# Attention outputs stored feature by feature, one pass that normalises them, and two modulation vectors of layer 0 formed on TensorE, in a two-layer hybrid encoder

## The chip, the cores and the metric

The kernel runs on one core of a Trainium2 chip. Its time is the device time of one execution in microseconds (us). The engines are TensorE (PE; its weight loads are PEld), VectorE (DVE), ScalarE (ACT), GpSimd (POOL) and SyncE (SP), which issues every DMA here.

## The reference, cut to what matters

Two sequences of 256 tokens with 1,024 features go through two layers. A layer modulates an RMS norm of x with vectors made from a conditioning vector c, projects it, and runs two groups of attention heads: group a has 8 query heads over 2 key and value heads of width 64, group b has 8 heads whose queries and keys are 96 wide, 64 without and 32 with a rotary position, the rotary key being shared by the heads. Each group's output (512 features) is RMS-normalised, and both go through one output projection. A channel mixer follows.

```
mod = silu(c) @ w_ada[l] + b_ada[l]                       # six vectors of 1024: shift, scale, gate, twice
h = rms_norm(x, g_attn) * (1.0 + scale_a) + shift_a
q_a, k_a, v_a, c_q, c_kv, k_r = split(h @ w_in)
o_a = softmax(q_a k_a^T * 64**-0.5) v_a                   # after head norm and rotation of q_a, k_a
q_b = rms_norm(c_q, g_cq) @ w_uq ; kv = rms_norm(c_kv, g_ckv) @ w_ukv
o_b = softmax([q_nope, rope(q_rope)] [k_nope, rope(k_r)]^T * 96**-0.5) v_b
x = x + gate_a * (concat(rms_norm(o_a, g_out_a), rms_norm(o_b, g_out_b)) @ w_o)
h = rms_norm(x, g_ffn) * (1.0 + scale_f) + shift_f
val, gate = split(conv3(h @ w_up)) ; x = x + gate_f * ((silu(gate) * val) @ w_down)
```

## The kernel before

**Numbers.** Each weight product is made of three one-pass matmuls (`product`, L614, L615, L620): a weight and an activation are each split into a rounded part, hi, and the remainder, lo, in the type fp32r. Attention itself runs on plain fp32 matmuls, which the trace shows as two matmuls and two weight loads each; a transpose is one.

**Weights.** SP loads 89 slots of 128 x 1,024 numbers a layer through a ring of four. ACT makes w_hi (L1117, `split_hi`), POOL makes w_lo in four quarters (L535), PE consumes. A slot of a ring is loaded again when POOL has read it and split again when PE has released it.

**Modulation vectors.** 11 vectors of 8 slots each are formed on DVE: a slot of `ada_raw` times silu(c), with a sum over its columns, for both sequences. A slot in full width takes two instructions (L1387), one in halves four (L1424). `ada_plan` says after which step of DVE's program how many slots are taken. Key ("unit", i) is unit i of the attention loop, ("wo", m) tile m of the output projection, ("up", g, i) and ("down", g, m) the tiles of the channel mixer, whose 22 tiles are in groups of 8, 8 and 6. SP loads slots of `ada_raw` through a ring of four of its own.

**Attention.** After the input projections, group b's queries are expanded token by token (L614 with ct_hi as the stationary operand, 384 columns), and their rotation is done by POOL (L579 to L588), which also copies the rotary key to all heads. Then 16 units follow, each of one pair of heads and one sequence: eight of group a, eight of group b. The loop keeps several units in flight. In a pass of it PE transposes the queries of the next unit (`fill`, L887 for a, L892 for b), multiplies them by the keys (`scores`, L917; for a the two heads use the upper and lower 64 rows of the array), transposes the probabilities of the unit before (`prob_transposes`, L931) and multiplies those of two units before by the values (`outputs`, L950). There the transposed probabilities are the stationary operand and the values move, 64 columns and one of ones, whose product is the sum of the exponentials. DVE takes the maxima (L1758) and divides the outputs by their sums (L1767, L1771). ACT copies the queries (L1278, L1280), takes the exponentials (L1307) and copies the transposed probabilities (L1296).

**End of attention.** `o_sb` is stored by token. ACT squares it by token (`stats`), DVE scales it, PE transposes it (L662), ACT and DVE split it into hi and lo (L1136, L1557), and `out_tile` multiplies it. Tiles 0 to 3 have 512 columns. Tiles 4 to 7 follow in halves by sequence (`norm_tail`), so that the sums of squares for the next norm hide behind them. DVE adds each tile to x (`update_x` L1593, `update_half` L1578) and sums the squares that ACT takes (`add_square`, L1570). A half needs a bank that an earlier update has freed.

**The order.** Each engine's program is written out by hand and the engines meet by semaphores; `plan_banks` deals the PSUM banks.

## Time and profile before

| | |
|---|---|
| median of 3 runs | 1193.37 us (1190.86 to 1193.6) |
| profiled execution | 1194.76 us, span 1193.0 us |
| mean granted TensorE clock | 0.986 of full speed |
| attention of layer 0, first query expansion to last 512-column output product | 91.6 to 223.5 us |
| the same of layer 1 | 670.5 to 792.1 us |
| DMA | 151.55 MB, mean 127 GB/s |

A busy share says how much of a stretch an engine had an instruction in flight. Matmuls overlap, so the spacing of their starts, and not their length, says what one costs. Where PE waited, its rows carry a bracket with the idle time and what ended it.

### The profile page before, as it was taken

To read this page: it belongs to the slowest core of one execution; us is meant where nothing else is said; L and a number is where in the kernel's file an instruction comes from. 1 tells how busy PE (TensorE), PEld (TensorE's weight loads), DVE (VectorE), ACT (ScalarE), POOL (GpSimd) and SP (SyncE) were. 2 spreads that over 40 slices of the span, in tenths; PEclk is the share of its full clock that TensorE was granted. 3 is DMA by queue.
4 is the path that set the end of the run, shared out by engine and by line. 5 is a ranking of instruction groups with operands and counts; after the bars stand their busy time and mean duration, and the time that the engine had idled before them with its cause. 6 is when DMAs were issued, how large, how long until landed. Compare 5 with 4: busy or idle time off the path is not lost.

```text
span 1193.0 us, 18770 instructions
## 1 busy us (share of the span) xinstructions
PE 1165.8 (98%) x6288; PEld 997.4 (84%) x6288; DVE 728.9 (61%) x1481; ACT 534.5 (45%) x866; POOL 568.4 (48%) x768
## 2 busy tenths in 40 slices
PE   9999999999999999999999999999999999999997
PEld 6897887998888888888789979889888888888886
DVE  5878986767766677757666438746775134412345
ACT  5347675254431344234354677635543234422432
POOL 2487500655655445644665540054555544454462
PEclk9999997999999999999999999999999999999998
DMA  9743333423445444544433202222343322332322
GB/s 350 307 168 116 92 103 107 141 72 132 174 139 207 133 166 176 194 141 176 141 110 119 75 1 89 89 89 71 124 141 106 106 86 90 106 106 74 102 89 71
DMA packets 43979, 151.55 MB, mean 127 GB/s; under 512 B 5122, under 2 KB 7810, under 8 KB 43908
## 3 DMA queue, kind: packets, MB, share of 16 engines
q1 hardware_dynamic: 43908, 150.64, 36.6%
q8 instruction: 40, 0.66, 0.2%
q14 instruction: 31, 0.25, 0.1%
HBM read 148.52 MB, written 2.10 MB: 126 GB/s over the span
## 4 chain that ended last, share of the span: by engine, by line
PE 46%; issue 24%; POOL 15%; POOLq 6%; DVE 6%; DVEq 2%; ACT 1%; ACTq 0%
POOL w_lo L535 14%; PE ps L614 14%; PE ps L620 14%; PE ps L615 14%; POOLq L536 5%; DVE ada_prod L1387 2%; DVEq L1389 1%; DVE nmx L1758 1%; PE ps L749 1%; PE ps L950 1%; PE ps L738 1%; PE ps L718 0%; DVE ada_prod L1608 0%; DVE o_sb L1771 0%; PE ps L726 0%
## 5 line engine op out<-in xcount | busy, mean ns | idle before, releaser
L535 POOL TENSOR_TENSOR w_lo<-w_raw,w_hi 128x256 fp32r<-128x256 f32 x712 | 532.1, 779 | 599.3 <-ACT w_hi L1117 575.7
L614 PE MATMUL ps<-h_hi,w_hi 128*128 128x512 f32 (+1 forms) x960 | 349.7, 364 | 4.2 <-DVEq L1561 2.2
L615 PE MATMUL ps<-h_lo,w_hi 128*128 128x512 f32 (+1 forms) x960 | 347.3, 362 | 0.0
L620 PE MATMUL ps<-h_hi,w_lo 128*128 128x512 f32 (+1 forms) x960 | 347.2, 362 | 0.0
L1117 ACT CAST w_hi<-w_raw 128x1024 fp32r<-128x1024 f32 x178 | 183.2, 1047 | 183.8 <-PE ps L614 183.6
L614 PEld LDWEIGHTS ps<-h_hi,w_hi 128*128 128x128 f32 x960 | 181.7, 189 | 36.8 <-DVEq L1561 3.8
L1809 DVE SCALAR_TENSOR_TENSOR u_sb<-ps,par,u_sb 128x510 f32<-128x510 f32 x176 | 131.7, 748 | 123.2 <-ACT u_sb L1345 110.2
L620 PEld LDWEIGHTS ps<-h_hi,w_lo 128*128 128x128 f32 x960 | 181.7, 189 | 27.5
L615 PEld LDWEIGHTS ps<-h_lo,w_hi 128*128 128x128 f32 x960 | 181.8, 189 | 27.2
L614 PE MATMUL ps<-a_hi,w_hi 128*128 128x512 f32 (+1 forms) x400 | 146.6, 366 | 3.3 <-DVEq L1595 2.4
L620 PE MATMUL ps<-a_hi,w_lo 128*128 128x512 f32 (+1 forms) x400 | 145.6, 364 | 0.0
L615 PE MATMUL ps<-a_lo,w_hi 128*128 128x512 f32 (+1 forms) x400 | 145.5, 364 | 0.0
L1424 DVE SCALAR_TENSOR_TENSOR ada_prod<-ada_raw,ps 128x512 f32<-128x512 f32 x192 | 124.2, 684 | 7.1 <-issue 0.9
L1345 ACT ACTIVATE u_sb<-ps,par 128x512 f32<-128x512 f32 x88 | 67.3, 773 | 109.0 <-PE ps L620 109.0
L1593 DVE SCALAR_TENSOR_TENSOR x<-ps,mod,x 128x256 f32<-128x256 f32 x96 | 42.1, 480 | 101.9 <-PE ps L620 100.8
L1387 DVE SCALAR_TENSOR_TENSOR ada_prod<-ada_raw,c_all 128x1024 f32<-128x1024 f32 x64 | 89.1, 1392 | 5.2 <-issue 1.2
L614 PEld LDWEIGHTS ps<-a_hi,w_hi 128*128 128x128 f32 x400 | 75.5, 189 | 17.9 <-issue 5.3
L620 PEld LDWEIGHTS ps<-a_hi,w_lo 128*128 128x128 f32 x400 | 75.5, 189 | 11.9
L615 PEld LDWEIGHTS ps<-a_lo,w_hi 128*128 128x128 f32 x400 | 75.5, 189 | 11.8
L1349 ACT ACTIVATE sil<-u_sb 128x512 f32<-128x512 f32 x44 | 27.8, 632 | 112.4 <-DVEq L1814 112.4
L614 PE MATMUL ps<-w_hi,h_hi 128*128 128x512 f32 (+2 forms) x192 | 67.2, 350 | 1.1 <-DVE h_lo L1651 0.9
L620 PE MATMUL ps<-w_hi,h_lo 128*128 128x512 f32 (+2 forms) x192 | 66.1, 344 | 0.0
(160 smaller groups left out, 1372.6 us busy)
## 6 DMA issues: line engine op xcount, KB each, us to landing
w_raw<-w_slots SPq DMA_DIRECT2D x178, 512.0 KB, 3.5
ada_raw<-ada_slots SPq DMA_DIRECT2D x88, 512.0 KB, 3.8
shift<-shift_slots SPq DMA_DIRECT2D x8, 512.0 KB, 13.2
x_tok<-x_rows SPq DMA_DIRECT2D x4, 512.0 KB, 9.6
x<-x_t SPq DMA_DIRECT2D x4, 512.0 KB, 13.7
y_t<-x SPq DMA_DIRECT2D x3, 512.0 KB, 2.9
y_t<-x SPq DMA_DIRECT2D x1, 256.0 KB, 3.0
y_t<-x SPq DMA_DIRECT2D x2, 128.0 KB, 2.7
```

The costliest lines, as they stand in the source:

```text
L535: nc.gpsimd.tensor_tensor(w_lo[:, j, c], w_raw[:, j, c], w_hi[:, j, c].bitcast(F32), ALU.subtract)
L536: nc.gpsimd.drain()
L614: hh = mm(out, stat[0], mov[0], start=first, stop=False)
L615: hl = mm(out, stat[0], mov[1], start=False, stop=False)
L620: return mm(out, stat[1], mov[0], start=False, stop=last)
L1117: nc.scalar.copy(w_hi[:, j, :], w_raw[:, j, :]).then_inc(hi_done, 1)
L1345: A(u_sb[:, e, half, :], ps[:, bank(key), :], ACT.Identity, bias=par[:, L, bass.ds(ft + PC_CB, 1)], scale=par[:, L, bass.ds(ft + (PC_CW + ...
L1349: A(sil[:, e, :], u_sb[:, e, 1, :], ACT.Silu).then_inc(sil_ready, 1)
L1387: V.scalar_tensor_tensor(out=ada_prod[:], in0=ada_raw[:, j % 4, :], scalar=1.0, in1=c_all[:, s, :], op0=ALU.mult, op1=ALU.mult, accum_out= ...
L1424: V.scalar_tensor_tensor(out=ada_prod[:, 512 * s:512 * s + 512], in0=ada_raw[:, q % 4, 512 * t:512 * t + 512], scalar=1.0, in1=ps[:, 6 + s ...
L1593: V.scalar_tensor_tensor(out=xs, in0=ps[:, bank(key), c], scalar=gate, in1=xs, op0=ALU.mult, op1=ALU.add)
L1809: V.scalar_tensor_tensor(out=u3[:, :, dst:dst + SEQ - 1], in0=p3[:, :, src:src + SEQ - 1], scalar=par[:, L, bass.ds(at + (PC_CW + tap * 2 ...
```

## The change

**Outputs by feature.** `outputs` swaps its operands: the values (64 columns) are stationary, the transposed probabilities move (256 columns), and the two heads of a pair use the left and right 64 columns of the array. The result has features in the partitions and is copied to `o_t` by DVE. The sums of the exponentials now come from ACT with each exponential (`accum_out`), and DVE divides the probabilities by them before they are transposed (`scale_rows`). A probability is transposed two passes after its scores, its output comes three passes after.

**One normalising pass.** POOL squares and adds `o_t` unit by unit; PE sums over partitions (`group_sums`), ACT takes roots, DVE inverts, PE spreads the result over all partitions (`group_spread`), DVE scales `o_t` once (`output_scaled`), ACT rounds, DVE subtracts. There is no transpose of outputs. Group a's part of output tiles 0 to 3 is multiplied ahead of group b's.

**Group b by feature.** Queries are expanded with the weights stationary (512 columns), with rotary columns and swapped ones beside each other; DVE multiplies these by a table. A score of group b is the sum of two matmuls of 64 rows each. The `fill` of group b and POOL's rotation are gone. The four rotary parts (kr_pad) are made by DVE.

**Modulation vectors.** The gate and shift of layer 0's attention and mixer (16 slots) are formed on PE in units 1 to 8 (`stream_products`: 32 stationary columns, four groups of columns; `stream_select`). The other slots move in the plan.

```diff
-ORDER = [(0, SCALE_A), (0, GATE_A), (0, SHIFT_F), (0, SCALE_F), (0, GATE_F),
+ORDER = [(0, SCALE_A), (0, SCALE_F), (0, GATE_A), (0, SHIFT_F), (0, GATE_F),
+READY = [(0, SCALE_A), (0, GATE_A), (0, SHIFT_F), (0, SCALE_F)] + ORDER[4:]
+STREAMED = (2, 3)
+N_PE = KD * len(STREAMED)
-HALVED = (4, 5, 6, 7, 8, 10)
+HALVED = (4, 5, 6, 7, 8, 9, 10)
...
-    plan = [(("in", 1), 6, 2), (("in", 2), S_UQ, 2)]
-    plan += [(("unit", i), S_WO - 1, 1) for i in range(NP + 1)]
-    plan += [(("wo", m), S_WO + m, 1) for m in range(1, TAIL)]
-    ups = [[1] * 8, [1, 2, 1, 2, 1, 2, 1, 1], [2, 2, 1, 1, 1, 0]]
+    plan = [(("in", 1), 6, 2), (("in", 2), S_UQ, 1), (("in", 3), S_UQ, 1)]
+    plan += [(("stream", i), S_WO - 1, 1) for i in range(N_PE)]
+    plan += [(("wo", m), S_WO + m, 1) for m in range(TAIL)]
+    ups = [[1, 2, 1, 2, 1, 2, 1, 2], [2, 2, 1, 2, 1, 2, 1, 2], [2, 2, 2, 2, 1, 0]]
...
-    plan += [((1, "unit", i), SLOTS + S_WO - 1, 1) for i in (7, 8, 9, 10, 11, 13, 14, 15)]
...
+                def add_squares(j):
+
+                    group, s, _ = PAIRS[j]
+                    k, c = pair_tile(j), slice(s * SEQ, (s + 1) * SEQ)
+                    total = (ssum if group == "a" else ssq_b)[:, c]
+                    pool.wait_ge(o_done, NP * L + j + 1)
+                    if k % 4 == 0:
+                        nc.gpsimd.tensor_tensor(total, o_t[:, k, c], o_t[:, k, c], ALU.mult)
+                    else:
+                        nc.gpsimd.tensor_tensor(o_sq[:, 0, :], o_t[:, k, c], o_t[:, k, c], ALU.mult)
+                        nc.gpsimd.drain()
+                        nc.gpsimd.tensor_tensor(total, total, o_sq[:, 0, :], ALU.add)
+                    nc.gpsimd.drain()
+                    pool.sem_inc(o_summed, 1)
...
+                for n in range(HEADS):
+                    j = slot(L, S_UQ + n // 4)
+                    key = ("uq", n)
+                    wait_free(pe, L, key)
+                    for k in range(2):
+                        at = (n % 4 * 2 + k) * P
+                        last = product(ps[:, bank(key), :], [r[:, j, at:at + P] for r in (w_hi, w_lo)],
+                                       [r[:, k, :] for r in (ct_hi, ct_lo)], k == 0, k == 1,
+                                       {0: 2, 4: 1}.get(n, 0) * int(k == 0))
+                    last.then_inc(full[bank(key)], 1)
...
+                        if group == "a":
+                            parts = [(q_t[:, j % 2, q * P:q * P + P], ka_t[:, c])]
+                        else:
+                            p, at = heads[0] // 2, s * SEQ + q * P
+                            parts = [(qn[:, p, at:at + P], kn[:, p, c]), (qr[:, p, at:at + P], kr_t[:, c])]
+                        for n, (st, mv) in enumerate(parts):
+                            for u in range(2):
                                 r = slice(64 * u, 64 * u + 64)
-                                st, mv = q_t[r, j % 2, 0, q * P:q * P + P], ka_t[r, s * SEQ:(s + 1) * SEQ]
-                            else:
-                                st = q_t[0:QK_B, j % 2, u, q * P:q * P + P]
-                                mv = kb_t[0:QK_B, heads[u], s * SEQ:(s + 1) * SEQ]
-                            last = mm(ps[:, S_BANK[j % 2] + u, q * SEQ:(q + 1) * SEQ], st, mv, start=True, stop=True)
+                                last = mm(ps[:, S_BANK[j % 2] + u, q * SEQ:(q + 1) * SEQ], st[r], mv[r], start=n == 0,
+                                          stop=n == len(parts) - 1)
...
+                    if L == 0 and j < 4 * len(STREAMED):
+                        stream_select(j)
                     pe.wait_ge(pt_ready, NP * L + j + 1)
-                    for u in range(2):
-                        for q in range(2):
-                            for k in range(2):
-                                v = va[:, 2 * s + k, u, :] if group == "a" else vb[:, 2 * s + k, heads[u], :]
-                                c = (2 * u + q) * VW
-                                last = mm(ps[:, O_BANK, c:c + VW], prob_t[:, j % 2, u, k, q * P:q * P + P], v,
-                                          start=(k == 0), stop=(k == 1))
+                    for k in range(2):
+                        for u in range(2):
+                            v = va[:, 2 * s + k, u, :] if group == "a" else vb[:, 2 * s + k, heads[u], :]
+                            last = mm(ps[64 * u:64 * u + 64, O_BANK, 0:SEQ], v, prob_t[:, j % 2, u, k, :],
+                                      start=(k == 0), stop=(k == 1))
                     last.then_inc(o_full, 1)
...
+                    pe.wait_ge(part_taken, h)
+                    for r in range(2):
+                        k = K_PE + 2 * h + r
+                        pe.wait_ge(ada_landed[k % 4], 16 * (k // 4 + 1))
+                        for g in range(4):
+                            last = mm(ps[32 * g:32 * g + 32, QT_BANK, 0:SEQ], c_pad[:, 4 * r + g, :],
+                                      ada_raw[:, k % 4, g * SEQ:(g + 1) * SEQ], start=r == 0, stop=r == 1)
+                        last.then_inc(ada_streamed, 1)
...
+                    pe.wait_ge(part_taken, h + 1)
+                    for f in range(2):
+                        at = h % 4 * 2 * NSEQ + f * NSEQ
+                        last = mm(stream_sums(h // 4)[:, at:at + NSEQ], part_sb(h)[:, f * P:f * P + P], sel, start=True,
+                                  stop=True)
+                    last.then_inc(stream_full, 1)
+
...
+                    if i == NP + 1:
+                        out_part(L, 0, (0, 1))
+                        group_sums(1)
                     if 0 <= i - 2 < NP:
-                        outputs(i - 2)
-                    if i >= NP:
-                        for k in range(2):
-                            output_transposes(L, 2 * (i - NP) + k)
-                for m in range(2):
-                    out_tile(L, m, range(KD // 2), int(m == 0))
-                for k in range(KD // 2, KD):
-                    output_transposes(L, k)
-                for m in range(2):
-                    out_tile(L, m, range(KD // 2, KD), int(m == 1))
-                for m in range(2, TAIL):
-                    out_tile(L, m, range(KD), 1)
+                        prob_transposes(i - 2)
+                    if L == 0 and 0 <= i - 1 < 4 * len(STREAMED):
+                        stream_products(i - 1)
+                out_part(L, 0, (2, 3))
+                group_spread(1)
+                outputs(NP - 1)
+                out_part(L, 1, range(KD // 2))
+                group_sums(2)
+                out_part(L, 2, range(KD // 2))
+                group_spread(2)
+                out_part(L, 3, range(KD // 2))
+                for m in range(TAIL):
+                    out_part(L, m, range(KD // 2, KD), int(m > 0))
                 norm_tail(2 * L + 1, lambda m, s, release: half_out(L, m, s, release))
...
-                split_hi(L, S_WO + 3)
+                              ACT.Exp, bias=nmx[:, i, c:c + 1], accum_out=rsum[:, i, c:c + 1]).then_inc(exp_ready, 1)
+                    if L == 0 and 0 <= i - 1 < 4 * len(STREAMED):
+                        act.wait_ge(ada_streamed, 2 * i)
+                        if i - 1 >= 3:
+                            act.wait_ge(stream_full, i - 3)
+                        nc.scalar.copy(part_sb(i - 1), ps[:, QT_BANK, 0:SEQ]).then_inc(part_taken, 1)
...
+            def output_scaled(L, e):
+
+                k, c, _, _ = event(e)
+                if e % (KD // 2) == 0:
+                    dve.wait_ge(group_full, 3 * L + e // (KD // 2) + 1)
+                V.scalar_tensor_tensor(out=o_t[:, k, c], in0=o_t[:, k, c], scalar=par[:, L, PC_GOUT + k:PC_GOUT + k + 1],
+                                       in1=sum_view(e // (KD // 2)), op0=ALU.mult, op1=ALU.mult).then_inc(on_ready, 1)
+
+            def output_lo(L, e):
+
+                k, c, hi, lo = event(e)
+                dve.wait_ge(on_hi_ready, N_EVENTS * L + e + 1)
+                V.tensor_tensor(lo, o_t[:, k, c], hi.bitcast(F32), ALU.subtract).then_inc(ot_ready, 1)
 
...
+                    dve.wait_ge(exp_ready, 4 * (NP * L + j + 1))
+                    V.reciprocal(rinv[:, j, :], rsum[:, j, :])
+                    V.drain()
+                    V.tensor_tensor(prob[:, j % 2], prob[:, j % 2],
+                                    rinv[:, j, :].rearrange("p (c o) -> p c o", o=1).broadcast_to([P, 4, SEQ]),
+                                    ALU.mult).then_inc(rows_scaled, 1)
...
+                    V.tensor_copy(o_t[:, k, c], o)
+                    V.drain()
+                    if L == 0 and j in STREAM_ENDS:
+                        take_stream(STREAM_ENDS.index(j))
+                    dve.sem_inc(o_done, 1)
+                    if j == NP - 1:
+                        V.tensor_tensor(o_sq[:, 1, :], o_t[:, k, c], o_t[:, k, c], ALU.mult).then_inc(last_sq, 1)
+
```

The instruction order shows three places. The first is TensorE in layer 0, a pass of the attention loop with a unit of group a. `ka_t` are keys, `q_t` queries, `va` values, `qb` group b's queries by token.

```order
L887 MATMUL ps<-ident,proj 128x128 x2
L917 MATMUL ps<-ka_t,q_t 128x256 x4
L931 MATMUL ps<-ident,prob 128x128 x8
L950 MATMUL ps<-va,prob_t 128x65 x8
L892 MATMUL ps<-ident,qb 96x128 x4
```

The same place now (L1058 are the products of the modulation weights, L1067 picks their rows):

```order
L983 MATMUL ps<-ka_t,q_t 128x256 x4
L954 MATMUL ps<-ident,proj 128x128 x2
L997 MATMUL ps<-ident,prob 128x128 x8
L1058 MATMUL ps<-ada_raw,ada_prod 32x256 x8
L1067 MATMUL ps<-scale_84,ada_prod 128x2 x2
L1016 MATMUL ps<-prob_t,va 64x256 x4
```

Eight output matmuls of 65 columns are four of 256, and ten matmuls for the modulation have come in between.

The second place is TensorE at the end of layer 0's attention, before:

```order
L931 MATMUL ps<-ident,prob 128x128 x8
L950 MATMUL ps<-vb,prob_t 128x65 x8
L662 MATMUL ps<-ident,o_sb 128x128 x8
L950 MATMUL ps<-vb,prob_t 128x65 x8
L662 MATMUL ps<-ident,o_sb 128x128 x8
L614 MATMUL ps<-h_hi,w_hi 128x512
```

and now, where `ga_hi` and `ga_lo` are the normalised outputs of group a and `ssq_b` the squares of group b:

```order
L1033 MATMUL ps<-ones,ssq_b 128x1 x2
L997 MATMUL ps<-ident,prob 128x128 x8
L1016 MATMUL ps<-prob_t,vb 64x256 x4
L687 MATMUL ps<-ga_hi,w_hi 128x512
L688 MATMUL ps<-ga_lo,w_hi 128x512
L693 MATMUL ps<-ga_hi,w_lo 128x512
```

Products of group a's outputs now stand between the last units.

The third place is VectorE in layer 0, the first tiles of the output projection, before:

```order
L1790 MEMSET ssum 128x512
L1593 SCALAR_TENSOR_TENSOR x<-ps,mod,x 128x256 x4
L1570 TENSOR_TENSOR ssum<-ssum,sq_x 128x512
L1387 SCALAR_TENSOR_TENSOR ada_prod,mod<-ada_raw,c_all 128x1024 x2
L1593 SCALAR_TENSOR_TENSOR x<-ps,mod,x 128x256 x2
```

and now:

```order
L1985 MEMSET ssum 128x512
L1703 SCALAR_TENSOR_TENSOR x<-ps,mod,x 128x256 x2
L1504 SCALAR_TENSOR_TENSOR ada_prod,mod<-ada_raw,c_all 128x1024 x2
L1703 SCALAR_TENSOR_TENSOR x<-ps,mod,x 128x256 x2
L1680 TENSOR_TENSOR ssum<-ssum,sq_x 128x512
```

A modulation slot (two instructions) now follows tile 0 too, so that four stand in these tiles where three stood.

## Rows read from the trace of the kernel before

**Rows 1.** The page, part 1: busy time, share of the span, instructions
```profile
PE 1165.8 (98%) x6288; PEld 997.4 (84%) x6288; DVE 728.9 (61%) x1481; ACT 534.5 (45%) x866; POOL 568.4 (48%) x768
```
**Rows 2.** Stretches: length, busy time by engine, granted clock, DMA share, GB/s
```profile
91.60:223.50 131.90, 126.42 (x774) 107.62 (x773) 108.95 (x197) 85.63 (x165) 51.44 (x54) 0.92 0.31 103
187.00:200.00 13.00, 12.77 (x53) 11.62 (x53) 7.37 (x16) 6.26 (x12) 0.00 (x0) 0.50 0.45 163
670.50:792.10 121.60, 118.01 (x776) 100.48 (x775) 68.86 (x146) 84.54 (x165) 34.59 (x50) 0.99 0.20 66
```
**Rows 3.** Timeline of TensorE, layer 1's attention: start, length, instructions
```profile
711.39 0.39 PE L887 MATMUL ps<-ident,proj 128*128 128x128 f32 x2
711.71 1.13 PE L917 MATMUL ps<-ka_t,q_t 64*128 64x256 f32 x8
712.77 1.09 PE L931 MATMUL ps<-ident,prob 128*128 128x128 f32 x8
713.70 1.90 PE L950 MATMUL ps<-va,prob_t 128*128 128x65 f32 x16
...
724.47 0.60 PE L892 MATMUL ps<-ident,qb 128*96 128x128 f32 x4
724.91 1.89 PE L917 MATMUL ps<-kb_t,q_t 96*128 96x256 f32 x8
726.64 1.04 PE L931 MATMUL ps<-ident,prob 128*128 128x128 f32 x8
727.51 1.90 PE L950 MATMUL ps<-va,prob_t 128*128 128x65 f32 x16
729.25 0.60 PE L892 MATMUL ps<-ident,qb 128*96 128x128 f32 x4
```
**Rows 4.** Timeline of TensorE, the matmuls by columns at the start
```profile
15.46 3.68 PE L726 MATMUL ps<-ones 128*64 128x256 f32 x16
19.08 2.17 PE L729 MATMUL ps<-ones 128*32 128x512 f32 x16
```
**Rows 5.** Weight loads of two lines: ns minimum/median/maximum, first and last start
```profile
L726 PEld LDWEIGHTS ps<-ones x16: 182/231/233, 15.5 to 18.1; 128*64 128x64 f32 x16
L718 PEld LDWEIGHTS ps<-ones x24: 186/333/339, 1.1 to 22.0; 128*128 128x128 f32 x24
```
**Rows 6.** Groups by line and form, whole span: busy us, mean ns, idle before
```profile
L1307 ACT ACTIVATE prob<-ps,nmx 128x256 f32<-128x256 f32 x128 | 50.3, 480 | 12.2 <-DVE nmx L1758 12.1
L1296 ACT COPY prob_t<-ps 128x1024 f32<-128x1024 f32 x32 | 32.4, 1012 | 15.6 <-PE ps L931 13.5 <-issue 0.6 <-PE ps L950 0.2
L1218 ACT ACTIVATION_READ_ACCUMULATOR junk<-ps 128x1 f32 x8 | 1.6, 196 | 0.0
L1758 DVE TENSOR_REDUCE nmx<-ps 128x4 f32<-128x1024 f32 x32 | 39.2, 1225 | 16.5 <-PE ps L917 13.7
```
**Rows 7.** Timeline of TensorE, output products of 512 columns, layer 1
```profile
791.62 0.39 PE L615 MATMUL ps<-h_lo,w_hi 128*128 128x512 f32 x1
791.84 0.39 PE L620 MATMUL ps<-h_hi,w_lo 128*128 128x512 f32 x1
```
**Rows 8.** Timelines of VectorE and GpSimd, output projection of layer 0
```profile
218.27 0.88 DVE L1593 SCALAR_TENSOR_TENSOR x<-ps,mod,x 128x256 f32<-128x256 f32 x2 [0.16 <-PE ps L620]
...
224.14 0.88 DVE L1593 SCALAR_TENSOR_TENSOR x<-ps,mod,x 128x256 f32<-128x256 f32 x2
...
231.44 0.48 DVE L1578 SCALAR_TENSOR_TENSOR x<-ps,mod,x 128x256 f32<-128x256 f32 x1
...
212.76 4.26 POOL L535 TENSOR_TENSOR w_lo<-w_raw,w_hi 128x256 fp32r<-128x256 f32 x4 [2.00 <-ACT w_hi L1117]
```
**Rows 9.** Timeline of VectorE, mixer tiles of layer 0
```profile
409.22 0.69 DVE L1822 TENSOR_TENSOR a_lo<-af,a_hi 128x512 fp32r<-128x512 f32 x1 [0.81 <-ACT a_hi L1351]
409.83 0.68 DVE L1424 SCALAR_TENSOR_TENSOR ada_prod<-ada_raw,ps 128x512 f32<-128x512 f32 x1
...
421.06 0.69 DVE L1822 TENSOR_TENSOR a_lo<-af,a_hi 128x512 fp32r<-128x512 f32 x1 [0.81 <-ACT a_hi L1351]
```

656 lines of the change are left out of this document (374 added, 282 removed).

## The prediction, made before the changed kernel ran

> **What bounds the kernel now.** I read the page's busy times first. TensorE is busy for 98% of the span [rows 1], so a change pays only where it shortens TensorE's program, fills a wait, or keeps the engine at full clock. Next come the stretches [rows 2]. From the first query expansion to the last 512-column output product, layer 0 takes 131.9 us and layer 1 takes 121.6 us. The same program is 10.3 us dearer in layer 0. The granted clock says why: 0.92 against 0.99 of full speed. From 187 to 200 us it is 0.50, the lower of the two levels (1.2 instead of 2.4 GHz). A share of full speed that is not granted is time lost to a TensorE that always has work: 131.9 x 0.08 = 10.6 us in layer 0, 1.2 us in layer 1. PE's idle time is 131.9 - 126.4 = 5.5 us in layer 0 and 3.6 us in layer 1.
>
> Then I read TensorE's timeline where nothing disturbs it [rows 3]. A fill of group a takes 0.32 us (711.39 to 711.71), scores of a 1.06, transposes of probabilities 0.93. A unit of b takes 0.44 for its fill, 1.73 for scores, 0.87 for transposes (727.51 less 726.64) and 1.74 for outputs, together 4.78 us without a gap. A unit of a, with the same outputs, is 4.05 us.
>
> **Attention on TensorE, by parts.** The concern is what the new forms cost.
> - Outputs: 8 fp32 matmuls of 65 columns, 1.74 us, become 4 of 256 columns in two groups of columns. One 256-column fp32 matmul that has the array to itself costs 1.73 / 4 = 0.43 us (scores of b), so four cost 1.73 one after the other. Scores of a are 4 such matmuls in two halves of the rows and take 1.06. For halves by columns there is one row: 16 instructions (8 matmuls) of 64 x 256 in 3.62 us to the next line's start [rows 4], 0.45 a matmul. That is either full clock and no overlap, or half clock and two at a time. The weight loads speak for the second [rows 5]: 128 columns take 186 ns at the least and 333 in the median at the start, 64 columns 182 at the least and 231 in the median. A load of half the columns at full clock should not take longer than 186. And the next line, four groups of 32 columns, does 8 matmuls of 512 columns in 2.1 us [rows 4], where one alone would take twice 0.43: more than three at a time. The granted clock does not show the half clock that early. So I take 1.06 us for outputs, and 1.73 as the other end.
> - Scores of b: 8 matmuls in halves of the rows, twice 1.06 less one change of mode (0.2), 1.92 us for 1.73. The fill of b goes, 0.44.
> - Query expansion: 48 one-pass matmuls of 512 columns at 0.227 us [rows 7] are 10.9 us, about 48 x 0.057 = 2.7 more than at 384. The transposes of outputs, 32 in each layer, go (32 x 0.116 = 3.7 us).
> - Layer 0's modulation products: 8 matmuls a unit in four groups of columns. The start has 8 of 512 columns in 2.10 us [rows 4]; half the columns, 1.05 us. The selection is 2 small fp32 matmuls, four instructions at 0.116, 0.46 us. In eight units 12.1 us.
>
> The sum at full clock for layer 0: 12.2 expansion with twelve transposes, 5.4 keys and values (24 x 0.227), 2.6 fills, 8.5 and 15.4 scores, 14.9 transposes, 17.0 outputs, 12.1 modulation, 2.0 sums and spreads (estimate, some 36 instructions at under 0.12 less overlap), 21.8 output products (96 x 0.227): 111.9 us. Layer 1, without the modulation: 99.8. To this I add what does not fit without a gap. A change of mode beside outputs and products at 0.2 each, 4.8 and 3.2 us. The start of the loop, where DVE now has four products of queries, four copies of keys and one of values in front of the first transposes, 3 and 4 us. The last units' chain from scores to outputs, 1.5 each. Layer 0 comes to 121.2, layer 1 to 108.5.
>
> **The other engines in a unit.** ACT's exponentials carry a sum: 4 x 0.39 (50.3 / 128) plus 4 x 0.20 for reading the accumulator = 2.4 us; with the copy of 1.01 [rows 6] and that of the queries (256 columns, an estimate of 0.39 by the exponential's) it is 3.8 us for a unit of a. PE has 3.6 there in layer 1, so ACT sets eight units, 2 us more: layer 1 is 110.5. DVE has 1.23 for the maxima [rows 6], some 1.4 for scaling 1,024 columns (twice the 0.69 of 512 [rows 9]), 0.5 for a copy and 0.2 for the reciprocals: 3.3 us, hidden. POOL has three quarters of a slot's 4.26 us, at most 3.2 [rows 8], hidden too.
>
> The gains are 131.9 - 121.2 = 10.7 us in layer 0, nearly all of it lost clock given back, and 121.6 - 110.5 = 11.1 in layer 1, from outputs (16 x 0.7), fills and the hidden normalisation.
>
> A rule of the Trainium skill speaks against the outputs: "TensorEngine Tiling (Array Packing)", section Key Properties, says that changing the tiling mode drains TensorE. By the trace's scores of a, a change costs some 0.2 us, and that is in the sum above; no run here shows one with columns in a loop.
>
> **What is given back: VectorE's slots.** The units took 17 + 8 slots of the modulation; 16 go to PE, and the mixer of layer 0 takes eight more, the output tiles one more.
> - Output tiles, layer 0. A tile with a slot takes DVE 5.87 us (218.27 to 224.14) [rows 8]. Before, tile 1 came to a DVE that had waited; three slots, the vector's last steps and then the first half update at 231.44. Now four tiles stand: 4.5 (without a square) + 3 x 5.87 = 22.1 us, and some 1 for the last steps, from the first full tile to the first half update. But PE has made group a's part earlier, so tiles fill 2.7 us apart (12 x 0.227) in place of 5.4. The fourth half needs the first half's bank, and PE comes to it 3 x 2.7 for the tiles and 3 x 2.9 for three halves (24 matmuls of 256 columns at a little over half of 0.227) = 16.8 us after the first full tile. DVE frees its bank at 23.2 to 24. PE waits 6.4 us at least. The same waits come by way of ACT, whose weight splits stand behind each square, and POOL's 4.26 us a slot; they overlap this one. I take 6.5, between 0 (if a gap absorbs it) and 10.
> - Mixer, layer 0. Two slots in a tile make DVE's step 11.84 us (409.22 to 421.06) [rows 9] against PE's 48 x 0.227 = 10.9. One slot less is 2.8 less (four times 0.68), so a lag of 0.95 is worked off by the next tile. The patterns 1,2,1,2 and 2,2,1,2,... hold. The last group, 2,2,2,2,1,0, arrives about 4 late at its fifth tile and 2 to 3 at its last, whose lo part PE needs at once: 2 us. Groups 1 and 2 end with two slots in front of the first down update, 2.8 us later than now; as each down tile gives 5.4 us of cover, I put 1 us each. With that 4.5 us, between 0 and 9.
> - A kernel that sits at half clock after these waits loses half of what it does there. Before, that took 10.6 us in layer 0. I put 3 us.
>
> The sum: -10.7 - 11.1 + 6.5 + 4.5 + 3.0 = -7.8 us. The profiled execution, 1194.8 us (span 1193.0), stands 1.4 above the median of 1193.4; minus 7.8 from the median gives 1185.6. I say 1186.
>
> **Rivals.**
> - *VectorE's backlog costs more.* Waits of 2.4 and 3.5 us in the output tiles bring the lower clock, as the waits at the end of attention did (13.0 us at 0.50): 6.5 more there, and the mixer's lag at its upper end, 4.5 more. Then 1186 + 11 = 1197, slower. It decides when DVE's first half update of layer 0 comes more than 10 us after PE wants its bank. For it: DVE's 22.1 us against 16.8 have no slack. Against: layer 1 has none of it.
> - *The column halves don't overlap.* Outputs then cost 1.73 + 0.2 and not 1.06: 0.85 x 32 = 27 us, of which ACT's slack in layer 1 hides 3. 1210, slower. Against it stand [rows 4, 5]. The skill's same page, section Gotcha 2: Feature Incompatibilities, says that column tiling excludes the fast weight load. By that rule the 231 ns would be full clock, and 8 loads of them 1.85 us, about the same time; the 182 ns of the shortest such load doesn't settle it.
> - *The backlog is absorbed.* ACT and POOL have room and the clock stays up: without the 3.0 and without 8 of the 11.0, 1186 - 11 = 1175.
> - *The change does not shorten a unit.* If the round from exponentials by DVE's scaling to the transposes sets the pace at 4.4 us in both groups, layer 1 gains 4 less and layer 0 2 less: 1192, no change. The loop's two passes of distance speak against it.
>
> **How the numbers follow.** The forecast has a chance of 0.46, with its own range of 1179 to 1193; the backlog 0.17; no overlap 0.08; absorbed 0.22; unit not shortened 0.07. 0.3%, 3.6 us, is about what a measurement of this kernel can tell from no change: 1189.8 to 1197.0. Of the forecast 0.37 lies below, 0.08 within, 0.01 above; absorbed is below (0.22); unit not shortened 0.01, 0.05 and 0.01; backlog 0.05 within and 0.12 above; no overlap above. Together faster 0.60, same 0.18, slower 0.22. The range for 8 in 10 is 1171 to 1203: it takes in both ends of the slots' costs, and leaves out the loss of overlap.
>
> **What would show it.** In the changed profile the output line should start to the next line within 1.0 to 1.3 us in a unit; 1.7 or more says no overlap. A unit of b should take 4.0 to 4.2 us in both layers, a unit of a 3.7 to 3.9 in layer 1 and 5.0 to 5.4 in layer 0. Layer 1's stretch should be 108 to 113 us, layer 0's 119 to 124 at a clock above 0.97. In layer 0 PE should wait for DVE or POOL in the halves of the output projection, 5 to 8 us, and in layer 1 not at all. The forecast is wrong if layer 1 gains under 6 us, or if layer 0 as a whole is shorter by over 8.

## The result, and the profile after

The changed kernel takes 1226.8 us (median of 4 runs, 1225.1 to 1230.1), the kernel before 1193.5: ratio 1.028, interval 1.025 to 1.032. I had said 1186, with 1171 to 1203 as the range for 8 in 10. The change is 33 us slower, and I was wrong in sign and by 41 us.

Part 1 of the page, as in [rows 1]:

```profile
PE 1161.8 (95%) x6264; PEld 962.5 (79%) x6264; DVE 745.4 (61%) x1491; ACT 515.8 (42%) x938; POOL 569.2 (47%) x783
```

With the span (1224.0 against 1193.0 us) and the mean granted clock of the run (0.973 against 0.986) this line gives an estimate of how the loss splits. TensorE idle: 1224.0 - 1161.8 = 62.2 us, before 1193.0 - 1165.8 = 27.2. Clock not granted: 1224.0 x 0.027 = 33.0 us, before 16.7. What is left, the work at full clock, is 1128.8 us, before 1149.1. By that the change took 20.3 us of work off TensorE, and brought 35.0 us of waits and 16.3 us of lower clock, together the 31.0 us between the spans. The waits are measured. The other two are too large, because a lower clock counts here even where it costs no time. Layer 0's input stage shows it, first after and then before, columns as in [rows 2]:

```profile
0.00:90.67 90.67, 88.40 (x496) 75.66 (x497) 68.34 (x128) 39.71 (x78) 45.34 (x61) 0.91 0.73 276
0.00:91.63 91.63, 89.39 (x497) 75.84 (x498) 64.91 (x128) 39.72 (x78) 45.47 (x62) 0.98 0.73 272
```

Its clock is 0.91 against 0.98, which the reckoning books as 6.3 us lost, and it is 1.0 us shorter. Without this stage the lower clock comes to 10 us and the work saved to 14.

The stretches, columns as in [rows 2]: attention of layer 0, its output projection in halves, the three groups of down tiles of its mixer, attention of layer 1.

```profile
90.67:227.09 136.42, 121.09 (x842) 86.99 (x841) 84.05 (x146) 75.82 (x203) 40.28 (x56) 0.96 0.25 90
227.09:282.59 55.50, 50.74 (x402) 49.70 (x401) 38.80 (x75) 23.22 (x41) 28.86 (x32) 0.97 0.35 124
348.12:400.26 52.14, 45.93 (x193) 36.96 (x192) 36.73 (x98) 13.42 (x15) 28.23 (x40) 0.97 0.50 179
487.30:539.32 52.02, 46.14 (x194) 37.66 (x193) 36.20 (x97) 12.12 (x14) 28.19 (x40) 0.93 0.49 172
604.60:647.44 42.84, 38.49 (x225) 33.46 (x224) 25.57 (x50) 20.32 (x31) 25.34 (x34) 0.92 0.35 123
702.57:822.27 119.70, 109.07 (x682) 79.73 (x681) 76.79 (x131) 75.08 (x197) 37.05 (x52) 0.96 0.07 25
```

The same down stretches before:

```profile
338.20:382.41 44.21, 43.80 (x193) 35.98 (x192) 29.09 (x78) 10.35 (x11) 23.77 (x34) 1.00 0.52 182
469.45:513.66 44.21, 43.80 (x193) 35.97 (x192) 31.22 (x84) 10.35 (x11) 26.68 (x38) 1.00 0.55 191
578.94:615.49 36.55, 35.28 (x226) 31.55 (x224) 20.88 (x38) 16.74 (x26) 21.47 (x28) 1.00 0.34 113
```

The down tiles hold the largest part: 7.9 + 7.8 + 6.3 = 22.0 us, with the same products. Layer 0's attention is 4.5 longer (131.9 before), its output projection 6.1 (49.4), layer 1's attention 1.7 shorter (121.4). What TensorE waited for, after (us in total, times, longest):

```profile
PE ps L687 <- DVEq L1705: 11.9, 5, 5.9
PE ps L687 <- POOLq L603: 8.1, 8, 2.3
PE ps L1043 <- DVE st_o L1658: 7.4, 2, 3.7
PE ps L1058 <- ACT q_t L1402: 6.9, 5, 1.4
PE ps L687 <- DVE ga_lo L1672: 5.5, 4, 2.2
```

Each is a place of its own. **In attention of layer 0**, TensorE's timeline of one unit of group a, and ScalarE's in the same time:

```profile
136.12 1.07 PE L1058 MATMUL ps<-ada_raw,ada_prod 128*32 128x256 f32 x16 [1.38 <-ACT q_t L1402]
137.13 0.61 PE L1067 MATMUL ps<-scale,ada_prod 128*128 128x2 f32 x4
137.66 1.08 PE L1016 MATMUL ps<-prob_t,va 128*64 128x256 f32 x8
138.68 1.13 PE L983 MATMUL ps<-ka_t,q_t 64*128 64x256 f32 x8
139.74 0.44 PE L954 MATMUL ps<-ident,proj 128*128 128x128 f32 x2
140.02 1.04 PE L997 MATMUL ps<-ident,prob 128*128 128x128 f32 x8
```
```profile
134.78 1.01 ACT L1393 COPY prob_t<-ps 128x1024 f32<-128x1024 f32 x1 [1.98 <-PE ps L997]
135.69 0.38 ACT L1402 COPY q_t<-ps 128x256 f32<-128x256 f32 x1
```

Outputs take 1.02 us from start to start (I had 1.06): the column halves overlap. Products take 1.01, the selection 0.53, scores 1.06; a unit of group b takes 3.97 in both layers (4.0 to 4.2 said). The forms cost what I said. But the products write the bank that holds the next unit's query fill, and ScalarE empties it only after the 1.01 us copy of the transposed probabilities. TensorE stands 1.38 us, and the unit takes 6.3 us (from 136.12 to the next products at 142.43), not 5.0 to 5.4.

**At group a's norms** (both layers): TensorE, ScalarE and VectorE.

```profile
178.04 2.06 PE L1043 MATMUL ps<-ident,st_o 128*128 128x128 f32 x8 [3.71 <-DVE st_o L1658]
```
```profile
176.22 1.28 ACT L1254 ACT_TABLE_LOAD   x1
177.51 0.26 ACT L1254 ACTIVATE st_o<-ps,eps 128x4 f32<-128x4 f32 x1
```
```profile
177.81 0.18 DVE L1658 RECIPROCAL st_o<-st_o 128x4 f32<-128x4 f32 x1 [2.52 <-ACT st_o L1254]
```

ScalarE comes to the roots only after a unit's exponentials, and loads a table of 1.28 us first. TensorE's spread of the inverse norms stands 3.71 us, and in layer 0 the spread and the first scores behind it run at half clock. The half clock also comes among group a's units, behind one of the waits of 1.38 us: the eight output instructions that take 1.08 us above take 1.95 here.

```profile
123.42 1.95 PE L1016 MATMUL ps<-prob_t,va 128*64 128x256 f32 x8
```

**In the mixer of layer 0**, VectorE's low parts (a_lo) of the first and last up tile of the first group, and the first down update, before and after:

```profile
273.43 0.69 DVE L1822 TENSOR_TENSOR a_lo<-af,a_hi 128x512 fp32r<-128x512 f32 x1 [0.81 <-ACT a_hi L1351]
...
343.25 0.69 DVE L1822 TENSOR_TENSOR a_lo<-af,a_hi 128x512 fp32r<-128x512 f32 x1 [0.81 <-ACT a_hi L1351]
...
348.60 1.87 DVE L1593 SCALAR_TENSOR_TENSOR x<-ps,mod,x 128x256 f32<-128x256 f32 x4 [1.24 <-PE ps L620]
```
```profile
283.13 0.69 DVE L2017 TENSOR_TENSOR a_lo<-af,a_hi 128x512 fp32r<-128x512 f32 x1 [0.81 <-ACT a_hi L1463]
...
358.66 0.69 DVE L2017 TENSOR_TENSOR a_lo<-af,a_hi 128x512 fp32r<-128x512 f32 x1 [0.80 <-ACT a_hi L1463]
...
364.90 1.87 DVE L1703 SCALAR_TENSOR_TENSOR x<-ps,mod,x 128x256 f32<-128x256 f32 x4
```

At the full tiles' step of 10.88 us, TensorE takes 7 x 10.88 = 76.2 us from the first to the last of eight tiles. Before, VectorE took 69.8: it came into the group some 6 us late (an estimate, since the first two tiles are made in halves) and worked that off with one slot a tile, in steps of 9.03 us. After, it took 75.5: with one and two slots in turn it works next to nothing off. Its last low part stands 10.5 us behind the start of the down tiles (348.12), where it stood 5.1 (338.20), and behind it come two slots, 5.5 us, in front of the first update. TensorE wants the bank:

```profile
365.95 0.77 PE L687 MATMUL ps<-a_hi,w_hi 128*128 128x512 f32 x1 [4.82 <-DVEq L1705]
```

The instruction is 0.77 us long where 0.39 is usual: half clock again, right behind the wait.

In the second and third group VectorE comes in on time and falls behind inside the group. The first and the last low part of the second, the wait behind it, and the last low part of the third:

```profile
416.20 0.69 DVE L2017 TENSOR_TENSOR a_lo<-af,a_hi 128x512 fp32r<-128x512 f32 x1 [0.81 <-ACT a_hi L1463]
...
495.70 0.69 DVE L2017 TENSOR_TENSOR a_lo<-af,a_hi 128x512 fp32r<-128x512 f32 x1 [0.82 <-ACT a_hi L1463]
...
504.22 0.76 PE L687 MATMUL ps<-a_hi,w_hi 128*128 128x512 f32 x1 [5.88 <-DVEq L1705]
...
617.14 0.69 DVE L2017 TENSOR_TENSOR a_lo<-af,a_hi 128x512 fp32r<-128x512 f32 x1 [0.81 <-ACT a_hi L1463]
```

A low part that is on time comes 5.1 us behind the end of its tile. The first low part of the second group does (416.20 against 400.26 + 10.88), as does the third group's. The last ones stand 8.4 us behind the start of the down tiles (487.30) and 12.5 (604.60), where they stood 6.4 and 6.2 before. A step of VectorE is not only its slots. Each time the vectors go over to the other half of c, two copies into PSUM come on top, so that a tile with two slots takes 13.2 us instead of 11.84:

```profile
419.61 1.29 DVE L1522 COPY ps<-c_all 128x512 f32<-128x512 f32 x2
```

In the third group TensorE waits for no bank. It waits 2.1 us for the last low part and 2.3 for GpSimd.

### The profile page after: what moved, and what is told of

It is laid out like the page before. It is cut to its first block, busy times and chain, and to the rows that moved or that the text cites. A ratio compares the mean times of both kernels' runs of the same rounds, so it can differ in the third digit from the quotient of the medians.

```text
span 1224.0 us, 18762 instructions
## 1 busy us (share of the span) xinstructions
PE 1161.8 (95%) x6264; PEld 962.5 (79%) x6264; DVE 745.4 (61%) x1491; ACT 515.8 (42%) x938; POOL 569.2 (47%) x783
## 4 chain that ended last, share of the span: by engine, by line
issue 34%; PE 33%; POOL 19%; POOLq 10%; DVE 2%; DVEq 0%; ACT 0%; ACTq 0%
POOL w_lo L600 19%; PE ps L687 10%; PE ps L688 10%; PE ps L693 10%; POOLq L602 7%; POOLq L660 2%; POOLq L658 1%; DVE ada_prod L1718 1%; DVE h_lo L1761 0%; PE ps L819 0%; PE ps L788 0%; PE ps L808 0%; DVE xn L1752 0%; PE ps L796 0%; DVE x L1651 0%
## 5 line engine op out<-in xcount | busy, mean ns | idle before, releaser
L687 PE MATMUL ps<-h_hi,w_hi 128*128 128x512 f32 (+1 forms) x864 | 316.8, 367 | 2.1 <-POOLq L603 1.9
L688 PE MATMUL ps<-h_lo,w_hi 128*128 128x512 f32 (+1 forms) x864 | 316.0, 366 | 0.0
L693 PE MATMUL ps<-h_hi,w_lo 128*128 128x512 f32 (+1 forms) x864 | 315.9, 366 | 0.0
L687 PEld LDWEIGHTS ps<-h_hi,w_hi 128*128 128x128 f32 x864 | 163.3, 189 | 29.2 <-POOLq L603 2.8
L693 PEld LDWEIGHTS ps<-h_hi,w_lo 128*128 128x128 f32 x864 | 163.2, 189 | 26.3
L688 PEld LDWEIGHTS ps<-h_lo,w_hi 128*128 128x128 f32 x864 | 163.2, 189 | 26.0
L687 PE MATMUL ps<-a_hi,w_hi 128*128 128x512 f32 (+1 forms) x400 | 149.8, 375 | 17.7 <-DVEq L1705 11.9
L1535 DVE SCALAR_TENSOR_TENSOR ada_prod<-ada_raw,ps 128x512 f32<-128x512 f32 x224 | 145.0, 684 | 8.0
L688 PE MATMUL ps<-w_lo,h_hi 128*128 128x512 f32 (+2 forms) x192 | 66.8, 348 | 0.0
```

The costliest lines, as they stand in the source:

```text
L687: hh = mm(out, stat[0], mov[0], start=first, stop=False)
L688: hl = mm(out, stat[0], mov[1], start=False, stop=False)
L693: return mm(out, stat[1], mov[0], start=False, stop=last)
L1535: V.scalar_tensor_tensor(out=ada_prod[:, 512 * s:512 * s + 512], in0=ada_raw[:, q % 4, 512 * t:512 * t + 512], scalar=1.0, in1=ps[:, 6 + s ...
```

## The experiments

Twelve kernels; ratios are to the kernel before, in the same rounds. Microseconds between two kernels are differences of medians, often from different rounds, and the kernel before stood at 1191.2 to 1194.6 in them; so what an edit did is read from the stages. The table has eight of the twelve. The lengths of the stages (us, from one mark of TensorE's timeline to the next; stages not shown differ by at most 0.6; the input stage of layer 0 varies by some 3 us without any edit to it, and that of layer 1 takes 55.1 or 56.7 whether or not slots are in it):

| | before | changed | fill first | spread late | mixer undone | mixer spread | in slots | all tail | slots l1 | gaps split |
|---|---|---|---|---|---|---|---|---|---|---|
| input 0 | 91.6 | 90.7 | 93.4 | 90.9 | 91.5 | 90.8 | 99.0 | 91.5 | 91.0 | 90.9 |
| attention 0 | 131.9 | 136.4 | 130.5 | 128.3 | 134.9 | 136.5 | 153.7 | 121.3 | 121.3 | 122.3 |
| projection 0 | 49.4 | 55.5 | 55.9 | 55.8 | 55.8 | 55.6 | 50.0 | 55.8 | 55.8 | 52.0 |
| down 0 | 44.2 | 52.1 | 53.0 | 53.1 | 44.2 | 44.7 | 52.0 | 44.7 | 44.2 | 44.2 |
| down 1 | 44.2 | 52.0 | 52.5 | 52.6 | 44.2 | 46.3 | 52.0 | 46.3 | 44.2 | 44.2 |
| down 2 | 36.6 | 42.8 | 42.9 | 42.9 | 36.7 | 38.8 | 42.9 | 38.8 | 36.6 | 36.6 |
| input 1 | 55.2 | 55.1 | 55.1 | 55.1 | 55.1 | 55.1 | 55.1 | 56.7 | 55.2 | 56.7 |
| attention 1 | 121.4 | 119.7 | 116.7 | 115.6 | 141.4 | 118.8 | 119.7 | 108.9 | 109.0 | 108.9 |
| projection 1 | 49.4 | 49.6 | 49.6 | 49.6 | 49.7 | 49.7 | 49.6 | 49.6 | 49.7 | 49.4 |
| span | 1193.0 | 1224.0 | 1219.5 | 1213.6 | 1222.9 | 1205.5 | 1244.0 | 1182.8 | 1176.7 | 1174.4 |

### The query fill before the transposed probabilities (`fill_first`)

```diff
+                    if i + 1 < NA:
+                        take_fill(i + 1)
                     if i >= 2:
                         take_transposes(i - 2)
-                    if i + 1 < NA:
-                        take_fill(i + 1)
```

> The changed kernel with one swap on ScalarE: in each pass of the attention loop it copies the query fill of the next unit before the transposed probabilities of the unit two behind, not after them. My theory: in group a TensorE's modulation products (layer 0) and scores (layer 1) wait for that copy, which stands behind a 1.01 us copy for no reason but the order. The five waits of 1.38 us in layer 0 and the 3.0 us in layer 1 should go, and a unit of group a in layer 0 should take 4.9 to 5.2 us where it took 6.3. Layer 0's attention goes from 136.4 to 127 to 130 us, layer 1's from 119.7 to 116 to 118, the kernel is 8 to 13 us faster than the changed one (1214 to 1219). Rival: the round of exponentials, scaling, transposes and their copy sets the pace of these units; then the wait moves from the products to the outputs, and the time stays within 2 us of 1226.8.

1220.0 us, ratio 1.021 (1.018 to 1.024), 6.9 us faster than the changed kernel. The waits for the copy are gone in both layers, and a unit of group a in layer 0 takes 4.86 us. Attention is 5.9 and 3.0 us shorter. It is less than forecast for layer 0, with the mean clock still at 0.95. The rival falls: no wait took the place of the old one in the steady units (one of 1.2 us came in an early unit of layer 0). In layer 1 a unit of group a now takes 3.34 us, without a wait for ScalarE:

```profile
728.78 1.13 PE L983 MATMUL ps<-ka_t,q_t 64*128 64x256 f32 x8
...
732.12 1.13 PE L983 MATMUL ps<-ka_t,q_t 64*128 64x256 f32 x8
```

ScalarE's exponentials, with the reading of their sums, start 0.46 us apart there.

### Group a's norms spread one unit later (`spread_late`)

```diff
-                    if i == NA + 4:
+                    if i == NA + 5:
                         group_spread(0)
```

> The changed kernel with the spreading of group a's inverse norms on TensorE one unit later. My theory: TensorE stands 3.71 us in each layer before it because ScalarE comes to the roots only after that unit's exponentials and then loads a table (1.28 us); one unit (3.97 us) later VectorE's reciprocal is there. The two waits go, and with them the lower clock behind them (some 2 us in each layer): 9 to 12 us faster than the changed kernel, 1215 to 1218. Rival: the chain behind it (scaled outputs, their high and low parts, first output tile) is the one that decides, and the 3.7 us come back as longer waits for the low parts at the first output products (2.2 us now): 0 to 3 us faster.

1215.8 us, ratio 1.020 (1.017 to 1.023), 11.0 us faster. Layer 0's attention is 8.1 us shorter, of which 3.7 is the wait; its clock is 1.00 where it was 0.96. Layer 1's is 4.1 shorter. The chain behind had room, all but 0.4 us in layer 0 and 1.2 in layer 1, by which other waits grew.

### The mixer's slots undone (`mixer_undo`)

```diff
-HALVED = (4, 5, 6, 7, 8, 9, 10)
+HALVED = (4, 5, 6, 7, 8, 10)
...
-    ups = [[1, 2, 1, 2, 1, 2, 1, 2], [2, 2, 1, 2, 1, 2, 1, 2], [2, 2, 2, 2, 1, 0]]
+    ups = [[1] * 8, [1, 2, 1, 2, 1, 2, 1, 1], [2, 2, 1, 1, 1, 0]]
+    plan += [((1, "unit", i), SLOTS + S_WO - 1, 1) for i in (7, 8, 9, 10, 11, 13, 14, 15)]
```

> The changed kernel with the old numbers of modulation slots in layer 0's up tiles (1 each in the first group) and eight slots back in layer 1's attention units, where the change took them out. My theory: VectorE enters each mixer group some 6 us late; with one slot a tile it works 1.9 us off per tile, with 1,2,1,2 nothing, so that the first down updates are 5 to 6 us late and TensorE waits and then runs at the lower clock. Undone, the three down stretches of layer 0 (52.1, 52.0 and 42.8 us) go back to 44.2, 44.2 and 36.6: 22 us. Layer 1's attention pays 8 x (3.3 + 2.6 - 3.97) = 15 us at most, 8 to 15. Together 7 to 14 us faster than the changed kernel. Rival: the late updates come from something else that the change brought (more half slots out of PSUM, or the late start after attention); then the down stretches stay above 48 us, and the kernel gets slower, by 5 to 10 us.

1226.6 us, ratio 1.029 (1.026 to 1.031), no change. The down stretches are those of before to 0.2 us; the fourth row is layer 1's attention:

```profile
347.52:391.74 44.22, 43.81 (x194) 35.96 (x193) 29.10 (x78) 10.37 (x11) 23.82 (x34) 1.00 0.51 181
478.78:522.99 44.21, 43.80 (x194) 35.96 (x192) 31.30 (x84) 10.38 (x11) 26.80 (x38) 1.00 0.54 191
588.27:624.99 36.72, 35.26 (x226) 31.56 (x224) 21.01 (x38) 16.77 (x26) 21.08 (x28) 1.00 0.34 113
680.12:821.56 141.44, 112.03 (x682) 81.66 (x681) 102.17 (x164) 75.86 (x197) 46.39 (x52) 0.92 0.15 51
```

So the eight slots in the mixer are the whole cause of its 22 us. In layer 1's attention the same eight slots cost 21.7 us, not my 8 to 15: TensorE idles 29.4 us there instead of 10.6, at a clock of 0.92. The new attention has no room on VectorE: moving the slots out of it was right, and where they went was wrong.

### The same 48 slots, spread otherwise in the mixer (`mixer_spread`)

```diff
-    ups = [[1, 2, 1, 2, 1, 2, 1, 2], [2, 2, 1, 2, 1, 2, 1, 2], [2, 2, 2, 2, 1, 0]]
-    downs = [[0, 1, 1, 1, 1, 1, 1, 1], [0, 1, 1, 1, 1, 1, 1, 1], [0] * 8]
+    ups = [[1] * 8, [1] * 8, [2, 2, 2, 1, 1, 0]]
+    downs = [[1, 2, 1, 2, 1, 2, 1, 2], [1, 2, 1, 2, 1, 2, 1, 2], [0] * 8]
```

> The changed kernel with the same 48 slots in layer 0's mixer, but one a tile in the first two groups of up tiles, 12 in each group of down tiles (1,2,1,2,...) and 2,2,2,1,1,0 in the last ups. My theory (VectorE's lag at the end of the up tiles is what TensorE waits for, not the number of slots): the down stretches fall from 52.1, 52.0, 42.8 to 44.2 to 46, 44.2 to 46 and 37 to 38; 17 to 22 us faster than the changed kernel, about 1207. Rival: the load itself is too much, for VectorE or because three transfers of 512 KB then fall into 5.44 us and GpSimd's splitting runs beside VectorE all the time; then TensorE waits for weights in the down tiles, and less than 8 us is gained.

1210.1 us, ratio 1.014 (1.012 to 1.016), 16.8 us faster with the same slots. The down stretches give back 17.2 of their 22.0 us: most of it is not the number of slots but VectorE's lag at the end of the up tiles. The waits that are left are short (0.7, 1.9 and 2.4 us of TensorE). The third down stretch is 38.8 us, not 37 to 38: the last ups took one slot more than before (with one less, in `slots_l1`, it is 36.6).

### The output tiles' slots in the input stage (`in_slots`)

```diff
-K_PE = KD + KD // 2
+K_PE = 2 * KD
-    plan = [(("in", 1), 6, 2), (("in", 2), S_UQ, 1), (("in", 3), S_UQ, 1)]
+    plan = [(("in", 1), 6, 2), (("in", 2), S_UQ, 3), (("in", 3), S_UQ, 3)]
-    plan += [(("wo", m), S_WO + m, 1) for m in range(TAIL)]
```

> The changed kernel with the four modulation slots of layer 0's output tiles moved to its input stage, before the attention (eight there instead of four). My theory: the output projection of layer 0 takes 55.5 us against 49.6 in layer 1, which has the same instructions and no slots, because the slots delay VectorE's updates, ScalarE's splits behind them and GpSimd's low parts, which take 5 us beside VectorE and 2.8 without. It should fall to 49.5 to 50.5 us. The input stage pays 0 to 8 us for four slots of 2.6 us each. Kernel 1221 to 1227. Rival: layer 0's projection is late for another reason (its tiles start before GpSimd's queue has caught up with attention); then it stays above 54 us and the kernel is at 1226 to 1234.

1244.4 us, ratio 1.043 (1.040 to 1.046), 17.6 us slower. The projection of layer 0 fell from 55.5 to 50.0 us: the slots are 5.5 of its 6.1. The low parts in GpSimd's timelines, with the changed kernel's slots and without any:

```profile
221.75 5.16 POOL L600 TENSOR_TENSOR w_lo<-w_raw,w_hi 128x256 fp32r<-128x256 f32 x4 [17.15 <-ACT w_hi L1243]
227.23 4.94 POOL L600 TENSOR_TENSOR w_lo<-w_raw,w_hi 128x256 fp32r<-128x256 f32 x4 [0.32 <-issue]
```
```profile
247.45 3.28 POOL L599 TENSOR_TENSOR w_lo<-w_raw,w_hi 128x256 fp32r<-128x256 f32 x4 [17.14 <-ACT w_hi L1242]
```

The price of the slots in the input stage was a miss, 25.6 us (8.3 there, 17.3 in the attention) and not 0 to 8. VectorE takes a slot in the time that I had put (2.6 us), but first stands 10.7 us for its load, and TensorE stands behind it:

```profile
117.50 1.23 DVE L1503 SCALAR_TENSOR_TENSOR ada_prod<-ada_raw,c_all 128x1024 f32<-128x1024 f32 x1 [10.69 <-DMA ada_raw<-ada_slots]
```
```profile
125.55 0.76 PE L686 MATMUL ps<-w_hi,ct_kv 128*128 128x512 f32 x1 [12.40 <-DVEq L1874]
```

### Three edits together (`all_three`)

> The changed kernel with three of the single edits together: the query fill before the transposed probabilities on ScalarE, group a's inverse norms spread one unit later, and the mixer's slots with one a tile in the up tiles. Alone they gave 6.9, 11.0 and 16.8 us. My theory: they are separate waits, so the sum holds, 34.7 us: 1192 (1188 to 1195), no slower than the kernel before. Rival: the waits share the same slack (an earlier attention only meets VectorE's backlog), and less than 28 us comes: over 1199.

The first two edits and the spread mixer: 1189.7 us, ratio 0.997 (0.995 to 0.999), 37 us faster than the changed kernel against 34.7 forecast. The waits are separate; the sum holds, and the changed kernel with three orders mended is no slower than the one before.

### The last transposes before the first output products (`all_tail`)

```diff
-                    if i == NP + 1:
-                        out_part(L, 0, (0, 1))
-                        group_sums(1)
                     if 0 <= i - 2 < NP:
                         prob_transposes(i - 2)
+                    if i == NP + 1:
+                        out_part(L, 0, (0, 1))
+                        group_sums(1)
```

> The three edits together, and TensorE's transposes of the last unit moved in front of the first output products. My theory: the wait of 2.2 us for the low part of group a's second tile, in each layer, is VectorE's (it scales the last unit's rows first), and the transposes are ready then: 2.2 us less in each layer, and part of the 6 us at the lower clock behind it: 3 to 8 us faster than without it, 1185 to 1189. Rival: the last units' chain (transposes, copy, outputs, copy, squares, norms of group b) decides, and the wait moves behind the outputs: within 1.5 us.

1186.4 us, ratio 0.995 (0.993 to 0.997), 3.3 us faster; the two attentions went from 124.9 and 111.1 us to these, columns as above:

```profile
91.54:212.82 121.28, 115.53 (x843) 84.17 (x841) 83.94 (x146) 76.62 (x203) 41.35 (x56) 1.00 0.30 101
672.65:781.55 108.90, 103.86 (x682) 76.79 (x681) 76.71 (x131) 75.28 (x197) 38.66 (x52) 1.00 0.09 27
```

121.3 and 108.9 us at full clock, 5.8 and 5.0 of them idle, stand against the 121.2 and 110.5 of the prediction.

### Slots in both input stages (`all_in`)

The same with `in_slots`, and with four of the mixer's slots in layer 1's input stage (`ups` of 8, 9 and 7 slots, two `downs` of 10).

> The same with the slots spread further: the four of layer 0's output tiles and four of its mixer's go to the input stages (eight in layer 0's, four in layer 1's), so that the mixer of layer 0 has 44 slots. My theory, VectorE's lag where it is waited for: layer 0's output projection 49.6 to 50.5 us, its down stretches 44.2, 44.2 to 44.5 and 36.6 to 37; the input stages pay up to 4 us each. 4 to 12 us faster than without it. Rival: VectorE's chain in the input stages has no room for a slot either, and each of the eight costs its 2.6 us: 20 us in, 10 us out, slower by 10.

1195.1 us, ratio 1.003 (1.001 to 1.004), a miss by 8.7 us the other way. The mixer and projection came out as said (44.2, 44.2, 36.5, 50.0), layer 1's input stage paid nothing (55.1), and layer 0's cost 22.7 us, in that stage and the attention behind it, as in `in_slots`. The rival had the size right and another reason, VectorE's room.

### Slots in layer 1's input stage alone (`slots_l1`)

The kernel of `all_tail` with the mixer's `ups` and `downs` of `all_in`, and:

```diff
+    plan += [((1, "in", 1), SLOTS + 6, 2), ((1, "in", 2), SLOTS + S_UQ, 1), ((1, "in", 3), SLOTS + S_UQ, 1)]
```

> The three edits and the moved transposes together, as the best so far (1186.4), and four of the mixer's slots in layer 1's input stage, where the run with both input stages used showed 55.12 us with them and 56.7 without; layer 0's input stage and output tiles keep the changed kernel's slots. My theory: the mixer of layer 0 falls from 44.7, 46.3 and 38.8 to 44.2, 44.2 and 36.5 (4.9 us), nothing is paid: 1180 to 1183. Rival: layer 1's input stage had room only because that run came to it with VectorE less behind; then it pays 2 us or more and the kernel is at 1184 to 1187.

1178.5 us, ratio 0.987 (0.985 to 0.989), lower than the 1180 to 1183 said. As the theory has it: all three down stretches are those of before, and nothing is paid. Of the 7.9 us against `all_tail`, 4.8 are the down stretches; 1.6 are layer 1's input stage at its shorter length, which the slots don't explain.

### Two slots in VectorE's gaps (`slots_gaps`)

Two of the four slots of the output tiles go before `group_inverse(L, 0)` and behind `group_inverse(L, 2)`.

> The same, and two of the four slots of layer 0's output tiles in two gaps of VectorE that the changed kernel's trace shows: before it inverts group a's norms (it waits 2.5 us there for ScalarE's roots) and before it scales the last sequence's outputs (2.9 us for TensorE). The other two stay behind the first two output tiles. My theory: layer 0's output projection falls from 55.8 to 49.6 to 51 us, its attention pays 0 to 2 us: 4 to 6 us faster than without it, 1175 to 1179. Rival: the gaps are shorter now that the other waits are gone, or TensorE waits for what VectorE does behind them; the attention then pays the 5.2 us of the two slots and nothing is won.

1181.4 us, ratio 0.989 (0.987 to 0.991): a miss, and 2.9 us above `slots_l1`, about what layer 0's input stage took longer (93.8 against 91.0). The projection fell only to 54.8 us. By the trace, two slots and the vector's last steps on VectorE delayed the third update, behind it ScalarE's square (idle 5.7 us), and behind that, in ScalarE's order, the split of weights that GpSimd waits for.

### The split before the square, with four slots (`l1_split`) and with two (`gaps_split`)

```diff
                 for e in range(N_UPD - 4):
-                    square(2 * L + 1, e)
                     if e < TAIL:
                         split_hi(L, S_WO + 4 + e)
+                    square(2 * L + 1, e)
```

> The run with four slots in layer 1's input stage (1178.5), and in the output projection ScalarE splits the next weights before it squares the updated tile, not after. My theory, read from its trace and the last one's: TensorE waits in layer 0's half tiles for GpSimd's low parts, which wait for ScalarE's splits, which stand behind squares that wait for VectorE's updates behind its modulation slots; besides, a low part takes 5.0 to 5.2 us beside a full slot and 3.3 without. The swap takes away the first, not the second: layer 0's projection goes from 55.8 to 52 to 54 us, layer 1's stays at 49.6; 2 to 4 us faster. Rival: GpSimd's 5 us each already set the pace from the first split; then less than 1 us.

1177.5 us, ratio 0.988 (0.986 to 0.990), the same within the measurement; the projection is 57.0 us, not 52 to 54. The rival is borne out: GpSimd's 5 us a slot set the pace from the first split. Its low parts follow each other at 0.3 us in both kernels, TensorE's wait for them shrinks only from 5.3 to 4.2 us, and one for VectorE's first half update appears, the one that my prediction had counted on:

```profile
227.72 0.35 PE L688 MATMUL ps<-ga_hi,w_hi 128*128 128x256 f32 x1 [2.22 <-DVEq L1691]
```

> The same swap on the run that has only two slots in layer 0's output tiles (54.8 us there). Its trace shows the third split 5.7 us late behind a square. My theory: with the swap all four low parts start as TensorE frees the slots, two of them take 5 us and two 3.3: the projection goes to 50 to 51.5 us and the kernel to 1175 to 1178. Rival: the updates themselves, or the second slot's last steps on VectorE, then hold TensorE by the banks: over 53 us, no gain.

1176.4 us, ratio 0.986 (0.984 to 0.988), with 52.0 us in the projection (54.8 without the swap), not 50 to 51.5. So ScalarE's order did hold the third split in `slots_gaps`. It is the lowest time, though it can't be told from `slots_l1`. GpSimd's low parts now start one behind the other, 5.17 and 4.42 us beside a slot and 3.27 without:

```profile
206.56 5.17 POOL L602 TENSOR_TENSOR w_lo<-w_raw,w_hi 128x256 fp32r<-128x256 f32 x4 [15.84 <-ACT w_hi L1245]
212.05 4.42 POOL L602 TENSOR_TENSOR w_lo<-w_raw,w_hi 128x256 fp32r<-128x256 f32 x4 [0.32 <-ACT w_hi L1245]
216.79 3.27 POOL L602 TENSOR_TENSOR w_lo<-w_raw,w_hi 128x256 fp32r<-128x256 f32 x4 [0.32 <-issue]
```

Both limits, VectorE's bank and GpSimd's 5 us, stand close together there. How the last 2.7 us against layer 1's projection divide between them was not tried.

## Why the prediction was wrong

By its own terms, predicted and measured on the profiled executions:

| term | predicted | measured |
|---|---|---|
| attention, layer 0 | -10.7 | +4.5 |
| attention, layer 1 | -11.1 | -1.7 |
| output projection, layer 0 | +6.5 | +6.1 |
| mixer, layer 0 | +4.5 (0 to 9) | +22.2 |
| lower clock behind the waits | +3.0 | in the rows above |
| all the rest | 0 | -0.1 |
| sum | -7.8 | +31.0 |

**The mixer, 17.7 us.** The step that failed is "a lag of 0.95 is worked off by the next tile. The patterns 1,2,1,2 and 2,2,1,2,... hold." It left out two things. It never asked whether VectorE is on time, and in the first group it is not: the first low part comes 0.54 us behind the start of the full up tiles, and the last one, which is on time, 5.05 behind the start of the down tiles, though the tiles lie a constant 10.88 apart. Before, a slot a tile left 1.9 us of slack, and that slack did work. And it left out VectorE's copies of the other half of c, 1.4 us each, and a vector's last steps. With them the pattern of the second group does not hold even for a VectorE that comes in on time: its seven steps take 79.5 us against 76.2, a lag of 3.3 where none was forecast. The third group ends 7.5 us late and not 2 to 3; only its 2 us of wait for the low part were right (2.1). Then "as each down tile gives 5.4 us of cover, I put 1 us each" for the two slots at the group's end: TensorE waits for the first update from the third down tile on, the lag stood in front of it, and the waits were 4.8 and 5.9 us with half clock behind them. `mixer_undo` shows that the eight slots are the cause (back to 44.2, 44.2, 36.7), `mixer_spread` that most of it is where they stand. How much of the rest is lag and how much the slots at the group's end was not tried apart.

**Attention, 15.2 and 9.4 us.** The work was forecast well. By the same estimate as above, layer 0's work at full clock is 136.4 - 15.3 idle - 5.5 clock = 115.6 us, against 111.9 + 4.8 = 116.7 predicted; layer 1's 119.7 - 10.6 - 4.8 = 104.3, against 103.0. What failed are the waits: 4.5 us in layer 0 and 7.5 in layer 1 (with ScalarE's bound) were put down, 15.3 and 10.6 came, and the clock that was to be "given back" was lost again behind them. I listed what ScalarE does in a unit and summed it (3.8 us), and did not lay its order against TensorE's. The period of 3.75 to 3.96 us in layer 1 looks like that sum, but it is luck: `fill_first` brings it to 3.34 with ScalarE's work unchanged, so the term "ACT sets eight units, 2 us more" was wrong too, with 0.59 us put for an exponential that takes 0.46. Two orders did it: the query copy behind the probabilities' copy, and the roots behind exponentials and a table load. With both mended and the last transposes moved, the two stretches are 121.3 and 108.9 us. The forecast's 121.2 and 110.5 are near those of the change with its order mended, not of the change as it stands. The prediction's own sign, a gain of under 6 us in layer 1, was met: it gained 1.7.

**The output projection** has the right size, and half the mechanism: in the changed kernel TensorE waits there for GpSimd alone (4.8 us in 5 waits). GpSimd's first low part starts behind ScalarE's split, the next three at its own 5 us. The wait for the bank shows only when that one is shortened (`l1_split`). I had named that way and set it beside the other as overlapping; it is the one that ended last.

**The rivals.** "VectorE's backlog costs more" (0.17) had the right engine and sign and mostly the wrong place: it stood on the output tiles, with 9 us in the mixer where 22 came, and gave 1197. "The column halves don't overlap" is refuted by 1.02 us an output. Here the Trainium skill's rule that a change of tiling mode drains TensorE ("TensorEngine Tiling (Array Packing)", section Key Properties) fits with what was put in for it: with 0.2 us at a change the sum is 116.7 us, within 1.1 of the 115.6 that the run gives by estimate. "Absorbed" is out by the result, "not shortened" by the 3.97 us of a unit of group b (4.78 before). All the cases together left nothing above 1210, since I took the waits as bounded by slots that move, and none of them could hold two waits that come from the order of a new loop.

## What to carry to other kernels

A pattern of extra work that just fits a period holds only for an engine that enters on time, and only if every step of it is counted: read its lag at the start of a stage and at the end, and count slack that works a lag off as in use. When a loop is written anew, lay each engine's order of one pass beside the others and follow every shared bank through it; sums of busy time per pass don't show a wait of 1.38 us that comes back in five units, or a table load in a chain. And price a wait on TensorE with the lower clock behind it: here 35.0 us of new waits brought some 10 us of it, by estimate.

## What the runs showed of the hardware

- Two column halves of 256-column fp32 matmuls overlap: four in 1.02 us in a loop, changes of form included, where one alone in the kernel before takes 0.43. Eight in four column groups take 1.01.
- A wait of 1.38 us a unit did not bring the lower clock for good: with these five waits in layer 0 the run with the later spread kept a mean of 1.00, while in the changed kernel (0.96) some instructions behind two of the five took twice their length. Behind waits of 3.7 to 5.9 us instructions at twice their length followed each time that I looked.
- GpSimd's low part of a weight slot took 5.17 us beside VectorE's full slots, and 3.3 without them; VectorE's instruction of 1,024 columns went from 1.23 to some 1.56 us beside it (1.55 to 1.58 in the output tiles of the changed kernel).
- The change of ScalarE from exponentials to roots cost 1.28 us each time.
